# Moving three activations and two turns one slot later in a two-block model kernel

## What is computed

```python
def ssd_branch(z, xbc, dt_raw, conv_w, conv_b, dt_bias, a_log, d_skip, norm_w, w_out):
    ...
    xbc = jax.nn.silu(depthwise_conv(xbc, conv_w, conv_b))
    xs, bs, cs = split_cols(xbc, (D_INNER, G * N, G * N))
    ...
    y = gated_rmsnorm(y.reshape(Bsz, S, D_INNER), z, norm_w)   # gates y with silu(z)

def window_attention(q, k, v, sink, rel_table):
    ...
    m = jnp.maximum(jnp.max(logits, axis=-1, keepdims=True), sink_l)
    p = jnp.exp(logits - m)
    p = p / (jnp.sum(p, axis=-1, keepdims=True) + jnp.exp(sink_l - m))
    out = jnp.einsum('bngrqk,bnkgd->bnqgrd', p.astype(v.dtype), vb)
```

## Time and profile before

| | before |
|---|---|
| median of 3 runs | 953.8 us |
| profiled execution, its own time | 954.24 us |
| its span | 952.4 us |
| busy share PE / DVE / ACT / POOL | 98% / 70% / 54% / 8% |
| granted TensorE clock | full in all 40 slices |
| weight load busy share | 85% |

### The profile page before, as it was taken

The page is one execution under the profiler, slowest core; times in us unless marked ns, Lnnn a source line. Parts: engine busy times, 40 slices in busy tenths (PEclk is TensorE's granted clock), DMA queues, the critical chain, the costliest instruction groups (busy, mean ns, idle before and its releaser), DMA issues.

```text
span 952.4 us, 13185 instructions
## 1 busy us (share of the span) xinstructions
PE 936.7 (98%) x5362; PEld 806.7 (85%) x5362; DVE 666.2 (70%) x915; ACT 511.0 (54%) x666; POOL 80.3 (8%) x76
## 2 busy tenths in 40 slices
PE   8999989999999999999999999999999999999998
PEld 7988879987888878888888888799888888888887
DVE  6779789988788764778776436777665768776433
ACT  6456886666545733465554335655563456554331
POOL 0102211023321000000000000700000000000000
PEclk9999999999999999999999999999999999999999
DMA  7843233554224385435445555863365445445541
GB/s 299 334 165 119 100 133 133 178 180 147 95 89 155 135 307 182 176 139 212 177 178 211 187 187 213 195 219 134 113 214 184 177 138 216 177 177 213 185 177 45
DMA packets 25276, 166.51 MB, mean 175 GB/s; under 512 B 2986, under 2 KB 3114, under 8 KB 6656
## 3 DMA queue, kind: packets, MB, share of 16 engines
q1 hardware_dynamic: 22464, 156.12, 45.5%
q0 software_dynamic: 2752, 9.54, 3.5%
HBM read 164.57 MB, written 1.08 MB: 174 GB/s over the span
## 4 chain that ended last, share of the span: by engine, by line
PE 82%; DVE 12%; ACT 4%; issue 2%; DMA 1%; SPq 0%; DVEq 0%; ACTq 0%
PE ps L390 53%; PE ps L614 11%; PE ps L616 6%; DVE conv_acc L1635 5%; DVE w_lo L1403 3%; ACT w_hi L1039 1%; PE ps L806 1%; PE ps L735 1%; PE ps L750 1%; PE ps L580 1%; DVE logit L1536 1%; PE ps L856 1%; DMA raw<-in_w_stream 1%; ACT ht L1062 1%; PE ps L815 1%
## 5 line engine op out<-in xcount | busy, mean ns | idle before, releaser
L1403 DVE TENSOR_TENSOR w_lo<-raw,w_hi 128x2048 fp32r<-128x2048 f32 x145 | 336.3, 2325 | 184.2 <-ACT w_hi L1039 184.2
L1039 ACT ACTIVATE w_hi<-raw 128x2048 fp32r<-128x2048 f32 x145 | 275.6, 1907 | 185.7 <-PE ps L390 168.8
L390 PE MATMUL ps<-w_hi,ht 128*128 128x512 f32 (+1 forms) x576 | 180.8, 388 | 0.0
L614 PE MATMUL ps<-ht,w_hi 128*128 128x512 f32 x448 | 158.4, 399 | 0.0
L390 PE MATMUL ps<-ht,w_hi 128*128 128x256 f32 (+1 forms) x816 | 150.0, 285 | 0.0
L390 PEld LDWEIGHTS ps<-ht,w_hi 128*128 128x128 f32 (+1 forms) x816 | 126.2, 190 | 3.0 <-issue 2.9
L390 PEld LDWEIGHTS ps<-w_hi,ht 128*128 128x128 f32 x576 | 107.3, 188 | 22.3 <-issue 0.7
L616 PE MATMUL ps<-ht,w_lo 128*128 128x256 f32 x448 | 125.8, 281 | 0.0
L390 PE MATMUL ps<-ht,w_lo 128*128 128x256 f32 (+1 forms) x408 | 115.2, 282 | 0.0
L390 PE MATMUL ps<-w_lo,ht 128*128 128x512 f32 (+1 forms) x288 | 110.5, 384 | 0.0
L614 PEld LDWEIGHTS ps<-ht,w_hi 128*128 128x128 f32 x448 | 84.2, 188 | 20.9
(11 more groups left out here) (299 smaller groups left out, 1229.4 us busy)
## 6 DMA issues: line engine op xcount, KB each, us to landing
raw<-in_w_stream SPq DMA_DIRECT2D x145, 1024.0 KB, 4.8
bias<-rel_scratch POOLq DMA_DIRECT2D x1, 3072.0 KB, 18.6
bias<-in_rpb POOLq DMA_DIRECT2D x16, 128.0 KB, 4.0
x_first<-in_x_in SPq DMA_DIRECT2D x2, 512.0 KB, 4.0
raw<-in_w_stream SPq DMA_DIRECT2D x2, 512.0 KB, 6.7
gates<-in_gate_bias POOLq DMA_DIRECT2D x4, 256.0 KB, 5.0
gates<-in_gate_bias POOLq DMA_DIRECT2D x2, 512.0 KB, 7.9
x<-in_x_in POOLq DMA_DIRECT2D x1, 1024.0 KB, 7.3
```

Of the source, the lines that this page charges most:

```text
L390: ins = pe.matmul(o, still, moving, start=first and n == 0, stop=last and n == 2, skip_group_check=True)
L614: pe.matmul(ps[:, b, :], hi[:, c], ht[:, :, k, :], start=opens and kt == 0, stop=False, skip_group_check=True)
L1039: act.activation(split_home(s)[0][:, 0:width(s)], raw[s % RAW_RING][:, 0:width(s)], ACT.Copy).then_inc(hi_ready, 1)
L1403: dve.tensor_tensor(lo[:, 0:width(s)], raw[s % RAW_RING][:, 0:width(s)], hi[:, 0:width(s)].bitcast(F32), ALU.subtract).then_inc(lo_ready, 1)
```

## The change

The silu of z's first chunk and of convolution chunks 0 and 1 move from slot 15 to slot 16 on ACT. The turns of chunks 0 and 1 move from slots 16 and 17 to slots 17 and 18, on PE, ACT and DVE. One thing is moved by a condition and not by the table: in a slot that is in `SILU_AT`, DVE runs `softmax_divide` after `conv_taps`, in another before it. Slot 15 is no longer in the table.

```diff
-TURN_AT = {16: 0, 17: 1, 20: 2, 21: 3, 22: 4, 24: 5}
-SILU_AT = {15: (0, 1), 19: (2, 3), 21: (4,), 23: (5,), 25: (6,)}
+TURN_AT = {17: 0, 18: 1, 20: 2, 21: 3, 22: 4, 24: 5}
+SILU_AT = {16: (0, 1), 19: (2, 3), 21: (4,), 23: (5,), 25: (6,)}
 TAPS_AT = {9: 0, 13: 1, 15: 2, 17: 3, 19: 4, 21: 5, 23: 6, 25: 7}
...
-                if s == 15:
+                if s == 16:
                     emptied(act, ("z", 0, 0)), emptied(act, ("z", 0, 1))
                     act.activation(zg(all_rows, 0, 512), zg(all_rows, 0, 512), ACT.Silu).then_inc(z_first_silu, 1)
```

## The result

The median of 20 runs is 955.51 us (954.22 to 958.68); the kernel before, run beside it 20 times, had 953.91 (953.61 to 956.04). The two medians are 1.6 us apart; the ratio of the runs is 1.0015, 95% interval 1.0009 to 1.0022, which is 1.4 us. That is slower beyond the noise, but by less than the 0.2% from which I call a change a change. The profiled execution took 954.96 us with a span of 953.2 us, before 954.24 and 952.4.

A forecast was written before the change was run, and what follows sets the result against it. PE, busy 98% of the span, was taken as the bound. PE's sum was -1.76 + 2.06 = +0.30 us, DVE's tables 0.52 late; the larger counts, so 953.8 becomes 954.3 us. Range 952.0 to 955.6.

The forecast's parts named there:

- rival 3: Slot 16 on ACT: the table load holds ACT 1.28 us longer than its row, time 955.6; chance 0.04.
- The first stall stays: PE's wait for DVE's `ot_lo` of step 5, before step 6's `prob_turn`, is untouched: cost 0.
- The second goes: PE's wait at step 6's `values1` for ACT's `prob_out` vanishes: gain 1.76 us.
- The silus are now in front of step 7's `prob_out`: ACT's longer chain in slot 16 delays step 7's `prob_out`; PE stalls 2.06 us at step 7's `values1`.
- Sum for PE: Second stall removed and new stall at step 7 added: -1.76 + 2.06 = +0.30 us.
- DVE's new order: Slot 15 divisors ahead of taps hidden; slot 18 copy waits for its turn, so DVE's tables start 0.52 us late.
- What becomes of it: From slot 18 on, the larger of PE's 0.30 and DVE's 0.52 arrives with no slack after: 0.5 us.
- The removed table loads: Two ACT loads go: one already in the second stall's sum, the one in slot 19 costed at nothing.
- Rival 1: Step 7's new stall does not come and the 1.76 us is kept: 952.0 us; chance 0.11.
- it costs nothing: Slot 15 divisors ahead of chunk 2's taps make step 6's `ot_lo` late, hidden by a cover of 4 us.

The follow-up runs named there:

- Experiment 7: Changed kernel with the silus of z's first chunk and chunks 0 and 1 in slot 17, turns in slots 18 and 19: 952.17 us, ratio 0.9971.
- experiment 10: The changed kernel a third time, no edit, beside the kernel before: 956.06 us median, ratio 1.0007.
- 8: Changed kernel with those silus in slot 17, turns in 18 and 19, and step 7's divisors behind chunk 2's first taps: 953.05 us, ratio 0.9985.
- 1: The changed kernel once more, no edit, beside the kernel before on the same chip: 956.36 us median, ratio 1.0014.
- 5: Changed kernel with eight matmuls, result never read, in slot 17 ahead of step 7's `values1`: 954.90 us median, ratio 1.0003.
- 9: Kernel before with seven matmuls, result never read, in slot 16 ahead of step 6's `values1`: 955.61 us median, ratio 1.0005.

## Why the prediction was right, and where not

The case was the forecast one: the stall went from step 6 to step 7, as the trace shows. The size was not. 955.51 us lies outside the 953.9 to 954.8 that the sum allowed itself, and 0.1 us inside the stated range, whose upper end was put at 955.6 for rival 3, a table load that holds ACT longer. That did not happen. So it is luck that the range held the time; what filled it is a clock that the sum does not know. Step by step:

- *The first stall stays*: 0.97, right. *The second goes*: right, `values1` of step 6 starts 3.46 us after the reference point, 3.54 forecast.
- *The silus are now in front of step 7's `prob_out`*: the stall is 1.94 and not 2.06. `prob_out` starts 12.07 after the reference point, 12.23 forecast: 0.08 of the difference was there before `ot_hi`, since `values1` of step 6 came earlier, and 0.08 is in the silus, `conv_in` and the first tap.
- *Sum for PE* 0.16, forecast 0.30. *DVE's new order*: tables 0.20 late, forecast 0.52. Half a slot was too long at 3.13; the turn in slot 18 comes 148.87 - 145.91 = 2.96 us into it. With no slack left, each of these tenths went straight into the sum, as the prediction had it.
- *What becomes of it*: the larger of the two terms arrives and nothing takes it up, as forecast, but it is 0.17 us at the mark of 412 us and not 0.5. The runs of the first result at 1.000 have a median of 954.39, 0.5 over the 953.91 of the kernel before; that fits 0.5 only by number, since the wait of the last section, in some runs and not in others, moves such medians by more.
- *The removed table loads*: nothing was gained by the one in slot 19. The load in slot 16 is 1.28 us long, starts 0.02 us behind `ot_hi`, and the silu starts 0.01 us behind it (131.11, 132.40), so the drain of the Trainium skill's page "ScalarE: Activation LUTs" is not in this trace either, and rival 3 did not happen.
- *Rival 1* needed `prob_out` 2.1 us earlier. Experiment 7 made it so by placing the silus one slot further, and got the 1.8 us.

Two steps were wrong. The first is a term that the sum does not have. I wrote the trace's clock of 1.00 into every piece and took a stall of 2.06 us as worth 2.06 us, no more than one of 1.76. At 1.94 it is followed by half clock in some runs, at a price of 1.6 us (experiment 10). The runs say how often: 33 of 43 runs of the change are at 0.998 or less and 32 of 94 of the kernel before. If 0.998 is one cut and 0.996 two (12 runs of the change, 5 of the kernel before), that is an estimate of 1.05 cuts a run against 0.39, and 0.65 more at 1.6 us make 1.0 us; by the mean clocks, 0.9979 and 0.9992 over 953 us, it is 1.2 us. With the 0.2 of the traces that is 1.2 to 1.4 us, where 1.4, 1.3 and 0.7 were measured. Filling the stall, whole or half, takes it away without touching ACT or DVE: 8 of 22 runs at 0.998 or less and mean clocks of 0.9991 and 0.9992.

The second is *it costs nothing* of the divisors ahead of the taps. For the sum that holds to 0.01 us. But it is that order which leaves the standstill in one piece of 1.94; with the old order it is 0.17 and 1.69, and the ratio falls from 1.0014 to 1.0001 on the same chip. That the division is the reason is not shown: five of its 12 runs are at 0.998 or less, nine of 12 of the change on that chip, too few to tell, and it was not tried apart from the order. With all in slot 17 the same order goes the other way: behind the taps is the slower one, and it has the more cuts, 4 runs of 12 against 1 of 13 (experiments 7 and 8).

Open: whether length alone decides. The 1.76 and 1.78 us stand in slot 16 and the 1.94 and 3.02 in slot 17, and no run has a standstill of 1.9 us in slot 16. Behind the wait of 1.5 us at 412 us two profiles have a cut, while filling the 1.76 us changed nothing. The three or four in ten of the kernels with shorter standstills may be the cuts at 412 us; no run tried that, and it does not explain why only one run in 13 has them with all in slot 17.

## What to carry to other kernels

Work taken out from in front of one consumer is put in front of the next one on the same in-order engine. Before moving it, read how far ahead of its consumer each later result is; here step 7 had 1.2 us of lead, which was no more than the way from `prob_out` to `values1` takes, and the move gave 1.76 and took 1.94. The gap in the row of the moved engine is where it belonged. In the kernel before, ACT stood idle in slot 17 for 2.65 us:

```profile
144.70 1.92 ACT L1039 ACTIVATE w_hi<-raw 128x2048 fp32r<-128x2048 f32 x1 [2.65 <-PE ps L390]
```

A standstill of PE can cost more than its length, and one profile at full clock does not show that. Read the granted clock of all runs and, where it is under 1.000, take a profile that has the cut; a few matmuls put into the stall, whose result nobody reads, tell whether the stall is behind the cuts, if there are enough executions to count them in (here 11 each, of which four against 33 of 43).

## What the runs showed that I had not expected

With 1.76 us of standstill in slot 16 the share of runs with a whole cut of the clock is 3 in 10, with 1.94 us in slot 17 it is 8 in 10, and with 3.02 us there all of them.

A second scatter of about 1.4 us exists at full clock. In the profiles of four of the twelve experiments (1, 5, 9 and 10), the kernel before among them with its stall filled, PE waits 1.4 to 1.5 us for `w_lo` at 618 to 620 us; the ten others, before and after among them, do not have it. In the profile after, which does not have it, the timelines of DVE and POOL read:

```profile
610.05 0.43 DVE L1880 TENSOR_TENSOR scale_row<-scale_row 128x256 f32<-128x256 f32 x1
...
610.98 9.64 POOL L2079 TENSOR_TENSOR bias<-bias,params 128x2048 f32<-128x2048 f32 x2 [6.08 <-DMA bias<-in_rpb]
```

In experiment 10, which has it:

```profile
610.86 3.59 DVE L1880 TENSOR_TENSOR scale_row<-scale_row 128x256 f32<-128x256 f32 x1
...
610.33 7.81 POOL L2079 TENSOR_TENSOR bias<-bias,params 128x2048 f32<-128x2048 f32 x2 [4.59 <-DMA bias<-in_rpb]
```

Where POOL's pass over `bias` starts first, a DVE instruction of 0.43 us takes 3.59, and the next pieces are late. Which of the two comes first hangs on when the last transfer of `bias` lands, which releases POOL. In all four profiles with the wait POOL was first, and in the ten others DVE. POOL's wait for the transfer is 4.3 to 4.7 us in the four and 5.8 to 6.3 in the ten. What makes it land earlier in some executions stays open. The slow taps of chunks 1 and 2 beside POOL's L2021 (4.86 us and not 3.25) fit the same exclusion. The Trainium skill has it in "SBUF — State Buffer", section "SBUF: two separate sides", as a lock on a port pair that the two engines share: a DVE instruction with two SBUF inputs or a POOL instruction that reads SBUF, whichever starts first, holds it for the whole instruction. Both rows agree: the 3.59 us end at 614.45, and the first half of POOL's 7.81 us at about 614.2.
